# Second-block FFN up-projections by one level of Strassen, weight sums on GpSimd, and the down-projection in three groups of FFN tiles

## The reference, cut to what matters

```
def _swiglu(h, w_gu, w_down):
    gate, up = jnp.split(h @ w_gu, 2, axis=-1)
    return (jax.nn.silu(gate) * up) @ w_down
...
    for l in range(DEPTH):
        x = _layer_norm(alpha * x + 0.5 * _swiglu(x, ffn_w_gu[l, 0], ffn_w_down[l, 0]), ln_g[l, 0], ln_b[l, 0])
        mix = _token_mixers(...)
        x = _layer_norm(alpha * x + mix, ln_g[l, 1], ln_b[l, 1])
        x = _layer_norm(alpha * x + 0.5 * _swiglu(x, ffn_w_gu[l, 1], ffn_w_down[l, 1]), ln_g[l, 2], ln_b[l, 2])
```

## Time and profile before

| what | value |
|---|---|
| median of 3 runs | 3473.43 us (3469.88 to 3474.93) |
| span of the profiled execution | 3466.1 us; its own time isn't listed apart from the three runs |
| PE busy | 3338.3 us, 96% |
| VectorE busy | 1787.2 us, 52% |
| ScalarE busy | 1399.9 us, 40% |
| GpSimd busy | 12.7 us |
| weight and table traffic | 284 MB on SP's queue, 82 GB/s over the span |
| mean granted clock of TensorE | 0.986 |

### The profile page before, as it was taken

The page is one execution under the profiler, slowest core; times in us unless marked ns, Lnnn a source line. Parts: engine busy times, 40 slices in busy tenths (PEclk is TensorE's granted clock), DMA queues, the critical chain, the costliest instruction groups (busy, mean ns, idle before and its releaser), DMA issues.

```text
span 3466.1 us, 46913 instructions
## 1 busy us (share of the span) xinstructions
PE 3338.3 (96%) x17496; PEld 2760.7 (80%) x17496; DVE 1787.2 (52%) x2538; ACT 1399.9 (40%) x2137; POOL 12.7 (0%) x13
## 2 busy tenths in 40 slices
PE   7999999999999999999999999999999999999997
PEld 6898888888788888888866778888888876688886
DVE  6573566537766534333586553335333567563335
ACT  5323344326544324222467442224222456642224
POOL 0000000000000000000000000000000000000000
PEclk9999999999999999999999999999999999999998
DMA  3110232222222222223211122222222211022223
GB/s 133 66 31 31 87 100 96 97 92 92 91 97 97 97 93 97 97 97 96 83 43 39 43 79 97 97 97 89 97 97 97 75 61 45 26 80 96 95 98 101
DMA packets 87432, 287.82 MB, mean 83 GB/s; under 512 B 9712, under 2 KB 11760, under 8 KB 86768
## 3 DMA queue, kind: packets, MB, share of 16 engines
q1 hardware_dynamic: 87136, 284.03, 24.6%
q0 software_dynamic: 144, 1.71, 0.1%
HBM read 283.61 MB, written 2.10 MB: 82 GB/s over the span
## 4 chain that ended last, share of the span: by engine, by line
PE 84%; DVE 9%; ACT 3%; issue 3%; DMA 1%; DVEq 0%; ACTq 0%; SPq 0%
PE gb L588 24%; PE gb L589 24%; PE gb L590 24%; PE gb L1256 2%; DVE wl L2038 2%; PE pm L1293 1%; PE pm L1273 1%; DVE rinv L2068 1%; DMA wst<-in_weights 1%; ACT wh L1417 1%; DVE work_a L2671 1%; DVE h L2054 1%; DVE xl L2092 0%; ACT work_a L1912 0%; DVE sq L2721 0%
## 5 line engine op out<-in xcount | busy, mean ns | idle before, releaser
L588 PE MATMUL gb<-xh,wh 128*128 128x512 f32 (+1 forms) x3168 | 1193.0, 377 | 51.9 <-DVE xl L2092 27.1
L589 PE MATMUL gb<-xl,wh 128*128 128x512 f32 (+1 forms) x3168 | 1170.6, 369 | 0.0
L590 PE MATMUL gb<-xh,wl 128*128 128x512 f32 (+1 forms) x3168 | 1170.2, 369 | 0.0
L2038 DVE TENSOR_TENSOR wl<-wst,wh 128x1024 fp32r<-128x1024 f32 (+2 forms) x584 | 643.4, 1115 | 439.2 <-ACT wh L1417 433.1
L1417 ACT CAST wh<-wst 128x1024 fp32r<-128x1024 f32 (+2 forms) x584 | 552.3, 960 | 594.5 <-DMA wst<-in_weights 594.0
L588 PEld LDWEIGHTS gb<-xh,wh 128*128 128x128 f32 x3168 | 607.5, 192 | 187.5 <-issue 54.4
L589 PEld LDWEIGHTS gb<-xl,wh 128*128 128x128 f32 x3168 | 608.2, 192 | 98.1 <-issue 4.8
L590 PEld LDWEIGHTS gb<-xh,wl 128*128 128x128 f32 x3168 | 607.7, 192 | 98.5
L588 PE MATMUL gb<-hid,wh 128*128 128x512 f32 (+1 forms) x1268 | 467.4, 369 | 2.0 <-DVE wl L2038 1.2
L590 PE MATMUL gb<-hid,wl 128*128 128x512 f32 (+1 forms) x1268 | 463.8, 366 | 0.0
L589 PE MATMUL gb<-hid,wh 128*128 128x512 f32 (+1 forms) x1268 | 463.7, 366 | 0.0
(11 more groups left out here) (402 smaller groups left out, 2950.5 us busy)
## 6 DMA issues: line engine op xcount, KB each, us to landing
wst<-in_weights SPq DMA_DIRECT2D x408, 512.0 KB, 3.3
wst<-in_weights SPq DMA_DIRECT2D x86, 384.0 KB, 2.9
wst<-in_weights SPq DMA_DIRECT2D x84, 320.0 KB, 2.9
h<-in_x_t SPq DMA_DIRECT2D x2, 1024.0 KB, 6.0
out_t<-h SPq DMA_DIRECT2D x8, 256.0 KB, 2.2
tab<-in_first SPq DMA_DIRECT2D x1, 1984.0 KB, 14.9
tab<-in_second POOLq DMA_DIRECT2D x1, 1666.0 KB, 7.4
wst<-in_weights SPq DMA_DIRECT2D x6, 256.0 KB, 2.6
```

What stands on the lines that cost most here:

```text
L588: pe.matmul(dst, w_hi, x_hi, start=start, stop=False)
L589: pe.matmul(dst, w_hi, x_lo, start=False, stop=False)
L590: return pe.matmul(dst, w_lo, x_hi, start=False, stop=stop)
L2038: dve.tensor_tensor(wl[:, s, m, a], wst[:, s, m, a], f32(wh[:, s, m, a]), ALU.subtract).then_inc(lo_split, 1)
```

## The change

The first two feature tiles stay as they are. The other 20 go in ten pairs `i` of tiles a and b (`u` is 0 or 1). For one tile the weights are a 2 x 2 block matrix: rows are gate and up, columns the two halves of the 1024 inputs (4 input tiles each); x is 2 x 2 as well, input halves by token halves. One level of Strassen in Winograd's form makes the four output blocks out of seven products P1 to P7, each of 4 input tiles by 256 tokens (12 matmuls with the three parts), instead of eight. Its weight operands are A1, A2 (gate) and A22 as loaded, and four sums V1 to V4 that GpSimd adds up (`block_sums`). Its x operands are the halves of x and three mixed ones, made at the start of the FFN by VectorE and ScalarE (`mixed`, `mixed_low`); the fourth takes the place of the first four tiles of `xh` and `xl` in the second token half.

The products land in PSUM in part on top of each other: P1, P6, P7, P4 in the "base" bank, P2 in the "side" bank, P5 and P3 in the "end" bank. Between them ScalarE copies what was reached (`side_copy` S, `snap` U2, `end_copy` E) and VectorE joins it (`c11`, `c22`, `c12`). Each engine has a written order, one for the first pair of a group and one for the others (`PE_ORDER`, `SUMS`, `HIGHS`).

The hidden tiles form three groups, 0 to 5, 6 to 13 and 14 to 21. After each group the down-projection of that group runs over all 8 output tiles, and VectorE adds it to `h` (`add_part`); the buffers of `hid` that a group leaves free hold the high and low parts of V and of the mixed x.

A pair's loads: the gate half of each tile goes to `wst`; the up half (the raw blocks) goes to `raw_blocks(u)`, one buffer for each of a and b. For the first pair of a group SP waits there until PE has used the chunk before (`chunk_done`), for the others until VectorE has split A22 of the pair before (`lo_split`). VectorE's `first_low` splits A1 and A2, and waits for the sums V2, V3 and V4 of its tile, as they read `wst`. P1 of a tile waits for `first_low` and for `group_free`, counted by `product` of the pair before.

The last group's down-projection holds what `ffn` had around output tiles 4 to 7 (shift, squares, sums). The first block's FFNs are unchanged.

```diff
-LAYER_C, LAYER_G = 2 * FF_C + M2_C, 2 * FF_G + M2_G
+GROUPS = ((0, 6), (6, 14), (14, 22))
...
+PAIRS = [(i, i == max(a // 2, 1), i == b // 2 - 1, r) for r, (a, b) in enumerate(GROUPS) for i in range(max(a // 2, 1), b // 2)]
...
+PE_ORDER = {True: "P1a P2a P5a P6a P1b P2b P7a P5b P6b P3a P7b P4a P3b P4b".split(),
+            False: "P1a P2a P1b P2b P6a P5a P6b P7a P5b P7b P3a P4a P3b P4b".split()}
+SUMS = {True: "V3a V2a V4a V1a V3b V2b V4b V1b".split(), False: "V1a V2a V3a V1b V2b V4a V3b V4b".split()}
+OPERAND = {"P1": "A1", "P2": "A2", "P3": "V4", "P4": "A22", "P5": "V1", "P6": "V2", "P7": "V3"}
...
+                def blocks(c, taken, first):
+                    sp.wait_ge(half_done, c0 + c - 1)
+                    sp.dma_start(wst[:, c % 2, 0, :], w_dram[c0 + c, 0]).then_inc(w_in[c % 2][0], 16)
+                    if first:
+                        sp.wait_ge(chunk_done, c0 + c - 1)
+                    else:
+                        sp.wait_ge(lo_split, 2 * (c0 + taken) + 3 + c % 2)
+                    sp.dma_start(raw_blocks(c % 2).rearrange("p a b -> p (a b)"), w_dram[c0 + c, 1]).then_inc(w_in[c % 2][1], 16)
...
+                c, g = c0 + unit_chunk(2 * i), (2 * l + f) * NPAIR + i - 1
+                for k, name in enumerate(SUMS[first]):
+                    v, u = name[:2], "ab".index(name[2])
+                    a_blocks = wst[:, u, 0, 0:BLK], wst[:, u, 0, BLK:]
+                    low_blocks = raw_blocks(u)[:, 0, :], raw_blocks(u)[:, 1, :]
...
+                        for m in range(2):
+                            pool.wait_ge(w_in[u][m], 8 * c + 16)
+                    if first and v == "V1":
+                        pool.wait_ge(chunk_done, c + u - 1)
+                    pool.wait_ge(S("prod"), 8 * g + 1 + COUNTED[prior].index(USED_BY[v] + name[2]))
+                    if v == "V1":
+                        x, y = low_blocks
+                    elif v == "V3":
+                        x, y = a_blocks[0], low_blocks[0]
+                    elif v == "V2":
+                        x, y = (block_raw("V3", u), low_blocks[1]) if first else (block_raw("V1", u), a_blocks[0])
+                        pool.wait_ge(S("v_sum"), 8 * g + 1 + SUMS[first].index(("V3" if first else "V1") + name[2]))
+                    else:
+                        x, y = block_raw("V2", u), a_blocks[1]
+                        pool.wait_ge(S("v_sum"), 8 * g + 1 + SUMS[first].index("V2" + name[2]))
+                    pool.tensor_tensor(block_raw(v, u), x, y, ALU.add).then_inc(S("v_sum"), 1)
...
+                run, part_run = 2 + 2 * l + f, 2 * l + f
...
+                def blocks(i, first, r):
...
+                    for name in PE_ORDER[first]:
+                        p, u = name[:2], "ab".index(name[2])
+                        v = OPERAND[p]
+                        if p == "P1":
+                            pe.wait_ge(lo_split, 2 * c + 1 + u)
+                            pe.wait_ge(group_free, g0 + j + u - 1)
+                            if first and r:
+                                pe.wait_ge(part_done, 2 * FT + 16 * part_run + 8 * (r - 1) + 7 + u)
+                        elif p == "P4":
+                            pe.wait_ge(lo_split, 2 * c + 3 + u)
+                            pe.wait_ge(up_joined, joined(g, first, "C22", u))
+                        elif p != "P2":
+                            pe.wait_ge(S("up_part"), 4 * FT + 8 * g + 1 + TURN[first].index(v + name[2]))
+                        if p == "P3":
+                            pe.wait_ge(S("v_hi"), high_of(part_run, i, first, "E" + "ab"[u]))
+                        elif p == "P6":
+                            pe.wait_ge(up_joined, joined(g, first, "C11", u))
+                        elif p == "P7":
...
+                        if i == 1 and p in ("P4", "P5", "P6", "P7"):
+                            pe.wait_ge(S("x_mix"), 2 * MIXES * part_run + MIXES + {"P5": 1, "P6": 2, "P7": 3, "P4": 5}[p])
+                        dst = side_of(u) if p == "P2" else end_of(u) if p in ("P5", "P3") else base_of(u)
+                        opens = p in ("P1", "P2", "P5")
+                        for k in range(KT // 2):
+                            col = slice(k * P, k * P + P)
+                            w_hi, w_lo = block_hi(v, u)[:, col], block_lo(v, u)[:, col]
+                            x_hi, x_lo = moving(p, k)
+                            pe.matmul(dst, w_hi, x_hi, start=opens and k == 0, stop=False, skip_group_check=True)
+                            pe.matmul(dst, w_hi, x_lo, start=False, stop=False, skip_group_check=True)
+                            mm = pe.matmul(dst, w_lo, x_hi, start=False, stop=k == KT // 2 - 1, skip_group_check=True)
...
+                def down(r, m):
...
+                def down_last():
...
+                def blocks(i, first, last, r):
...
+                            act.wait_ge(chunk_done, c + u - 1)
...
+                            act.wait_ge(S("v_sum"), 8 * g + 1 + SUMS[first].index(name))
+                            act.copy(block_hi(v, u), block_raw(v, u)).then_inc(S("v_hi"), 1)
...
+                    def end_copy(u):
+                        act.wait_ge(S("prod"), 8 * g + 9 + COUNTED[first].index("P5" + "ab"[u]))
+                        act.wait_ge(hid_lo, run * FT + j + u - 1)
+                        act.copy(xf[:, u, HI_TOKENS], end_of(u)).then_inc(S("v_hi"), 1)
...
+                    else:
+                        high("V2a")
+                        high("V1a")
+                        side_copy(0)
+                        high("V2b")
+                        high("V3a")
+                        side_copy(1)
+                        snap(0)
+                        end_copy(0)
+                        high("V1b")
+                        high("V3b")
+                        snap(1)
+                        high("V4a")
+                        end_copy(1)
+                        high("A22a")
+                        high("V4b")
+                        high("A22b")
+                    n_cols = (GROUPS[r][1] - GROUPS[r][0]) * P if last else COLS
+                    split_half(c + 2, 0, 0, n_cols)
+                    gate_out(j)
+                    hid_high(j)
+                    split_half(c + 2 if last else c + 3, 0 if last else 1, 1 if last else 0, n_cols)
+                    gate_out(j + 1)
+                    hid_high(j + 1)
...
+                def product(j):
...
+                    dve.wait_ge(up_act, e + 1)
+                    if j < 2:
+                        dve.scalar_tensor_tensor(xf[:, s, :], sq[:, s, :], 0.5, gb[:, 2 * s + 1, :], ALU.mult, ALU.mult).then_inc(group_free, 1)
+                    else:
+                        dve.wait_ge(up_joined, joined(part_run * NPAIR + j // 2 - 1, STARTS[j // 2], "C22", s))
+                        dve.scalar_tensor_tensor(xf[:, s, HI_TOKENS], sq[:, s, HI_TOKENS], -0.5, xf[:, s, HI_TOKENS], ALU.mult, ALU.mult)
+                        dve.wait_ge(chunk_done, c0 + unit_chunk(j) + 1)
+                        dve.scalar_tensor_tensor(xf[:, s, LO_TOKENS], sq[:, s, LO_TOKENS], -0.5, base_of(s), ALU.mult, ALU.mult).then_inc(group_free, 1)
+                    dve.wait_ge(group_free, g0 + j + 1)
...
+                def first_low(c, u, g, first):
+                    dve.wait_ge(S("v_sum"), 8 * g + 1 + max(SUMS[first].index(v + "ab"[u]) for v in ("V2", "V3", "V4")))
+                    dve.wait_ge(hi_split, 2 * c + 1 + u)
+                    dve.tensor_tensor(wl[:, u, 0, :], wst[:, u, 0, :], f32(wh[:, u, 0, :]), ALU.subtract).then_inc(lo_split, 1)
...
+                    else:
+                        low("V2a")
+                        c11(0)
+                        low("V1a")
+                        c11(1)
+                        low("V2b")
+                        low("V3a")
+                        low("V1b")
+                        low("V3b")
+                        low("V4a")
+                        low("A22a")
+                        c22(0)
+                        low("V4b")
+                        low("A22b")
+                        c22(1)
+                        c12(0)
+                    product(j)
+                    n_cols = (GROUPS[r][1] - GROUPS[r][0]) * P
+                    if last:
+                        split_half(c + 2, 0, 0, n_cols)
+                    else:
+                        first_low(c + 2, 0, g + 1, False)
+                    hid_low(j)
+                    c12(1)
+                    if last:
+                        split_half(c + 2, 0, 1, n_cols)
+                    else:
+                        first_low(c + 2, 1, g + 1, False)
+                    product(j + 1)
+                    hid_low(j + 1)
...
+                def add_part(r, m):
...
+                def mixed(t):
+                    b11, b12, b21, b22 = (h[:, k:k + 4, v] for k in (0, 4) for v in (LO_TOKENS, HI_TOKENS))
+                    if t == 1:
```

(71 more changed lines are left out.)

361 lines of the change are left out of this document (330 added, 31 removed).

## The result

The changed kernel takes 3830.66 us (median of four runs, 3826.32 to 3833.48), the kernel before on the same chip 3471.65: ratio 1.1033, 95% interval 1.1018 to 1.1049. That is 359 us slower. I forecast 3810, within 3680 to 3910. Times of versions are medians too, and a lap is the time from one P1a to the next. The span went from 3466.1 to 3830.0 us.

The account below looks back on a forecast made before the run. PE's matmuls were taken to bound the kernel before (busy 3338.3 of 3466.1 us). Pairs +333, down-projection -2 and +8 gave +339; 3466.1 + 339 + 7.3 = 3812, stated as 3810 us, range 3680 to 3910.

Parts of the forecast that it names:

- What a product is worth: Up-projection matmuls: 0.1199 us for 256 columns, 0.2267 for 512; a feature tile 10.08 instead of 10.88 us, at best 64 saved.
- The ring: Inside a group: A22a's split, raw load, six GpSimd sums, first_low, next P1a take 14.0 us; period 31.3 instead of 21.8.
- the turn: At first_low of tile a: VectorE and GpSimd's V3b take turns at the ports, so first_low loses 1.3 us.
- The clock: Behind each PE pause of 9 us: the granted clock falls to 0.50, so P1a and P2a take 5.1 us.
- One FFN: All ten pairs of an FFN, by groups: 300.8 us for what takes 217.6, +83.2 an FFN, +333 in all.
- The down-projection and the tail: Down-projection: -2 us for products no longer halved, +8 for last sums some 2 us late, nothing for earlier groups' adds.
- Light: Rival: the weights' load-and-sum chain binds, but ports and clock cost next to nothing; 3640 to 3740 us, chance 0.19.
- Heavy: Rival: GpSimd slowed in most sums, or the clock low through much of each pair; above 3900 us, chance 0.11.
- Faster: Rival: load and sums end before PE runs dry, A22a's split to next P1a under 6.7 us; about 3415, chance 0.04.
- No change: Rival: the pair's period comes to 21.5 us by chance, total within 0.2% of the kernel before; chance 0.01.

Follow-up runs that it names:

- noload: Changed kernel, raw second halves of the weights loaded only for the first pair of each group, other pairs only raising the count: 3622.88 us.
- early: Changed kernel with the casts and subtractions of A22a and A22b some 9 us sooner in the pairs that aren't first: 3643.36 us.
- twice: Changed kernel with GpSimd doing the sum V3a twice in every pair that isn't the first of its group: 3871.40 us.
- turn: Changed kernel with GpSimd waiting for first_low of tile a before it starts V3b, in pairs that aren't first: 3811.70 us.
- warm: Changed kernel with 36 extra matmuls of 512 columns ahead of P1a in every pair that isn't the first of its group: 3808.75 us.
- Cover: Kernel before, with the sums of the first half behind 17 of the last output tile's 22 input tiles in place of 6: 3491.11 us.
- groups: Changed kernel with hidden-tile groups (0,8), (8,16), (16,22) in place of (0,6), (6,14), (14,22): 3856.92 us.

## Why the prediction held, and where it was off

**What a product is worth.** Right: the pitch of 256 columns at full clock is 0.12 us, as the earlier trace rows have it, and a pair that nothing stalls takes 20.25 us (noload; forecast 20.2). In the changed kernel the last pairs of their groups, with the lower clock at their start, took 21.8, 22.1 and 21.6 us (forecast 22.7): the clock and the wait for P1b eat the gain, and two tiles cost what they cost before.

**The ring.** Right in each link, off in two small ones. A22a's split 17.1 us after P1a (17.3); load and start 4.2 us (3.4; the likely reason is that two raw loads and one of a first half stand together, where the raw ones take 4.7 us to land and the other 5.3, against medians of 3.7 and 3.3 over the span); six sums 7.7 (7.6); the turn about 1 (1.3); the sum 14.4 (14.0); periods 32.0, 31.5, 30.75 and 30.6 (31.3). That it is a ring, early and noload show; that each sum counts, twice; the turn, turn.

**The clock.** Right: half clock for 3 to 6 us behind each pause (forecast 5.1), 0.8 us a lap (warm).

**One FFN.** In the first, pair 1 38.6 (37.2), pair 3 33.4 (34.8), pair 7 37.2 (35.5). All pairs 299.5 (300.8): +81.9 an FFN for +83.2. The other three have 299.2, 301.4 and 299.7.

**The down-projection and the tail: the term that was mis-sized.** "The last sums come some 2 us late: +8 us in all", and nothing for the groups. By landmarks in the trace the first FFN is 89.7 us longer (four times that is 359); 81.9 are pairs, so 7.8 are the rest: +31 us where I had +6. 2.4 of them lie in the first two down-projections, with a wait for hid's low half at their start (1.32 us in the first). Some 5.4 are the tail. I priced the squares' lateness and forgot that the last output tile's second half is also the cover of the normalisation behind the sums: 36 matmuls of 256 columns fewer, 4.3 us, an FFN. Cover shows that on the kernel before, and groups the same pause on the changed one. What is left of the tail wasn't split up.

**The rivals.** Light (3640 to 3740) failed in its time, though it was nearer than I had it on its reason: turn and warm put ports and clock at 19 and 22 us, 41 of 359. Heavy failed: the sums ran undisturbed at 1.26 us but for the last, because VectorE waited. Faster failed by the distance that it named: 14.4 us against 6.7. No change failed with it. The remark that the ports alone wouldn't let a pair go under today's 21.8 held for the laps of noload and of early and was too mild; that it is the ports, and they alone, is read from the lengthened operations and wasn't tested by itself.

In sum 81.9 x 4 = 328, and 31: 359. The forecast had 333 and 6. The term for the pairs came out right within 2%, and nearly all of its terms held; the 25 us too few for the rest is the error that remains, and the 5 too many for the pairs hide a little of it. That part is luck.

## What to carry to other kernels

When a change feeds a buffer from work that itself waits on the buffer's last reader, write the lap down (last use, split, load, preparation, first use) and compare it with the work that it must hide under; busy shares don't show it. If it is too long, move the last reader's split ahead in the engines' orders first: that was worth 187 us here, against 27 for the first pairs' loads and 22 for the clock. And when the last stage of a projection is cut into fewer input tiles, count what it covered behind it.
